# A two-stage sequence model in one launch: norm chains with a joint Ln/Exp table set, norms in pieces, and modulation units at other places

## The reference, cut to what matters

```python
def first_block(x, ...):                      # x: 1 x 256 x 1024
    h = x
    for l in range(DEPTH):                    # DEPTH = 2
        u = _rmsnorm(h, norm_mix_g[l])
        (s_z, s_xbc, s_dt, g_q, ..., gates) = _split(u @ w_in[l], IN_SIZES)
        ...                                   # three branches, gated and merged
        h = h + merged @ w_out[l]
        u = _rmsnorm(h, norm_ffn_g[l])
        up = _dwconv(u @ w_up[l], ffn_conv_w[l], ffn_conv_b[l])
        h = h + (silu(a_half) * v_half) @ w_down[l]
        h = h + (p[l] @ w_ple[l]) * sigmoid(h @ w_ple_gate[l])
    return _rmsnorm(h, final_norm_g)

def second_block(x, c, ...):
    # modulation: sh1, sc1, g1, sh2, sc2, g2 = split(silu(c) @ w_ada + b_ada, 6)
    h = rms_norm(x, norm1_g) * (1 + sc1) + sh1
    ...                                       # differential attention and pooling, out product
    x = x + g1 * mix
    h = rms_norm(x, norm2_g) * (1 + sc2) + sh2
    y = hierarchical_moe(h, ...)              # 32 experts in 4 groups, top 2
    x = x + g2 * y
    return rms_norm(x, final_g)
```

## Time and profile before

| | |
|---|---|
| time, median of 3 runs | 2242.56 us (2238.19 to 2245.31) |
| profiled execution, first to last instruction | 2239.7 us |
| TensorE matmuls busy | 2032.3 us (91%) |
| VectorE busy | 1202.3 us (54%) |
| ScalarE busy | 902.2 us (40%) |
| DMA | 499.45 MB, mean 223 GB/s |
| mean granted clock of TensorE | 0.956 |

### The profile page before, as it was taken

One profiled execution on the slowest core, in us unless ns is written; L12 is line 12 of the kernel. 1 busy time (PEld: TensorE's weight loads), 2 busy tenths in 40 slices (PEclk: granted clock), 3 DMA queues, 4 the chain that ended last, 5 costly groups with the idle time before them and its releaser, 6 DMA issues.

```text
span 2239.7 us, 47727 instructions
## 1 busy us (share of the span) xinstructions
PE 2032.3 (91%) x20606; PEld 1722.9 (77%) x20606; DVE 1202.3 (54%) x2113; ACT 902.2 (40%) x1088; POOL 30.9 (1%) x61
## 2 busy tenths in 40 slices
PE   8999999989999999999999999999897767777775
PEld 7998858889999989988588899999776533343433
DVE  4887856388677557878563886775233200000001
ACT  5554533474555455545334755554312200000001
POOL 0000000000000000000000000000000000000000
PEclk9999999999999999999999999999998898878878
DMA  6554333445445554553334454556662699999996
GB/s 254 183 204 178 132 113 133 160 160 189 169 178 187 202 196 175 208 184 132 114 132 160 160 182 165 182 188 226 249 242 94 276 421 422 422 422 422 422 422 259
DMA packets 70920, 499.45 MB, mean 223 GB/s; under 512 B 8320, under 2 KB 8448, under 8 KB 12016
## 3 DMA queue, kind: packets, MB, share of 16 engines
q1 hardware_dynamic: 66240, 481.41, 56.2%
q0 software_dynamic: 4384, 14.75, 1.9%
q10 hardware_dynamic: 144, 1.05, 0.1%
HBM read 496.03 MB, written 1.15 MB: 222 GB/s over the span
## 4 chain that ended last, share of the span: by engine, by line
PE 69%; DMA 14%; DVE 6%; ACT 5%; SPq 3%; issue 2%; DVEq 0%; ACTq 0%
PE bank L863 25%; PE bank L868 12%; DMA ring<-stream 11%; PE bank L873 9%; DMA arena<-stream 4%; SPq L715 3%; PE bank L1102 3%; PE bank L806 2%; PE bank L851 2%; PE bank L818 2%; PE bank L1320 2%; PE bank L856 1%; PE bank L1217 1%; PE bank L1075 1%; PE bank L924 1%
## 5 line engine op out<-in xcount | busy, mean ns | idle before, releaser
L873 PE MATMUL bank<-u,ring 128*128 128x256 f32 x1152 | 256.2, 381 | 0.0
L2241 DVE TENSOR_TENSOR ring_r<-ring,weights_and_u_split 128x2048 fp32r<-128x2048 f32 x88 | 201.6, 2292 | 94.0 <-ACT weights_and_u_split L1680 90.3
L873 PEld LDWEIGHTS bank<-u,ring 128*128 128x128 f32 x1152 | 216.9, 190 | 30.2 <-issue 0.8
L2556 DVE COPY arena<-bank 128x128 f32<-128x128 f32 x32 | 9.3, 292 | 401.8 <-PE bank L1338 401.8
L868 PE MATMUL bank<-weights_and_u_split,ring_r 128*128 128x256 f32 x1592 | 208.9, 283 | 0.0
L1680 ACT ACTIVATE weights_and_u_split<-ring 128x2048 fp32r<-128x2048 f32 x88 | 167.8, 1908 | 96.5 <-PE bank L868 52.6
L863 PE MATMUL bank<-weights_and_u_split,hidden_and_weights_high 128*128 128x256 f32 x1600 | 202.1, 284 | 0.0
L863 PEld LDWEIGHTS bank<-weights_and_u_split,hidden_and_weights_high 128*128 128x128 f32 x1600 | 195.4, 192 | 4.7 <-issue 4.3
L868 PEld LDWEIGHTS bank<-weights_and_u_split,ring_r 128*128 128x128 f32 x1592 | 199.0, 192 | 0.0
L2241 DVE TENSOR_TENSOR ring_r<-ring,hidden_and_weights_high 128x2048 fp32r<-128x2048 f32 x60 | 137.0, 2287 | 33.5 <-ACT hidden_and_weights_high L1680 33.5
L1320 PE MATMUL bank<-ring,arena 128*32 128x256 f32 x1008 | 90.6, 489 | 58.9 <-DMA ring<-stream 58.9
(11 more groups left out here) (407 smaller groups left out, 3491.8 us busy)
## 6 DMA issues: line engine op xcount, KB each, us to landing
ring<-stream SPq DMA_DIRECT2D x329, 1024.0 KB, 4.8
arena<-stream SPq DMA_DIRECT2D x128, 1024.0 KB, 26.2
arena<-rows_scratch POOLq DMA_DIRECT2D x48, 256.0 KB, 4.1
h<-x_d ACTq DMA_DIRECT2D x1, 1024.0 KB, 5.5
out<-arena SPq DMA_DIRECT2D x1, 1024.0 KB, 3.9
con<-con_d SPq DMA_DIRECT2D x1, 976.5 KB, 12.6
arena<-con_d POOLq DMA_DIRECT2D x1, 848.0 KB, 7.1
par<-par_d POOLq DMA_DIRECT2D x2, 422.0 KB, 4.6
```

The costliest lines, as they stand in the source:

```text
L873: mm = pe.matmul(bank[:, c * S:(c + 1) * S], w[:, k, c * P:(c + 1) * P], x[:, k, :], start=(k == 0), stop=(k == KC - 1))
L2241: tt(ring_r[:, POS[k] % RING, :], w, high(k).bitcast(F32), ALU.subtract).then_inc(wlo_ok.sem, 1)
```

## The change

It has five parts.

1. `prime` no longer computes anything: it loads the table set that holds both Ln and Exp. Neither the dummy nor a load between Ln and Exp is left in the program.
2. x comes in four loads with semaphores of their own. The ring's first load waits for the second of them. The first table load waits for nothing but `eps`.
3. Squares and sums of layer 1's first norm, and of the second block's first norm, are made in pieces among the four pleg units ("next_square", "next_sum"). Of the third norm in the second block two of four sums stand ahead of the last unit. At the end squares follow the h adds by pairs and the output is stored in two DMAs.
4. The weight copy of z0 stands ahead of u's parts, which are an item of their own ("parts").
5. Pair 0 of the modulation units moves behind z1, with SiLU of c behind z0's read, and pair 2 moves from bm's start to the end of the layer, behind the last pleg unit.

```diff
@@ unit_order
-    out, mk, bh, o = [ADA1, ADA1 + 1], OF["mk"], OF["bh"], OF["out"]
+    out, o = [], OF["out"]
...
-        if n == OF["gh"] + 3:
+        if n == OF["z"] + 1:
+            out += [ADA1, ADA1 + 1]
+        elif n == OF["gh"] + 3:
             out += [ADA1 + 2, ADA1 + 3]
-        elif n == bh + 3:
-            out += [ADA1 + 4, ADA1 + 5]
...
-    return out
+    return out + [ADA1 + 4, ADA1 + 5]
@@ sched
-        sched = [("norm", 0), ("ada", 0), ("ada_read", 0), ("split", 1), ("unit", 0), ("ada_cols", 0), ("lb", 0), ("split", 2), ("rows", 0)]
+        sched = [("norm", 0), ("split", 1), ("parts", 0), ("unit", 0), ("lb", 0), ("split", 2), ("rows", 0)]
...
+            if n == 1:
+                sched.append(("silu_c", 0))
             if n == 2:
-                sched.append(("keep_h", 0))
+                sched += [("ada", 0), ("ada_read", 0), ("keep_h", 0)]
+            if n == 3:
+                sched.append(("ada_cols", 0))
...
                 sched.append(("ple_add", n - pleg))
+                if n > pleg:
+                    sched.append(("next_sum", n - pleg - 1))
+                sched.append(("next_square", n - pleg))
+        sched += [("ada", 2), ("ada_read", 2), ("next_sum", 3), ("ada_cols", 2)]
@@ sync
-                    sp.wait_ge(x_in, 16)
+                    sp.wait_ge(x_in[1], 16)
...
-                sp.wait_ge(y2_fin, 2)
-                sp.dma_start(out, flat(0, KC)).then_inc(stored, 16)
-                sp.wait_ge(stored, 16)
+                for n in range(2):
+                    sp.wait_ge(y2_fin, 5 + n)
+                    sp.dma_start(out[:, n * 4 * S:(n + 1) * 4 * S], flat(4 * n, 4)).then_inc(stored, 16)
+                sp.wait_ge(stored, 32)
@@ tensor
+            def norm_sum(lay, before, j):
+
+                pe.wait_ge(sq_ready.sem, sq_ready.at(lay, before + j + 1))
+                for c in (2 * j, 2 * j + 1):
+                    mm = pe.matmul(A[4][:, 0:S], ones, arena[:, SQ + c, :], start=(c == 0), stop=(c == KC - 1))
+                if j == 3:
+                    mm.then_inc(ss_ready.sem, 1)
...
                 out_products(m, heads, False, True)
+                if m > WOUT2:
+                    norm2(3, [m - WOUT2 - 1])
             gemm2(WOUT2 + 3, chunks(O2, KC))
-            norm2(3)
+            norm2(3, (2, 3))
@@ scalar
             def prime():
 
-                act.activation(small[:, 255:256], eps[:, 0:1], ACT.Ln)
+                act.preload_act_table_set("natural_log_exp_and_others")
...
-            act.dma_start(h[:].rearrange("p c s -> p (c s)"), x_d).then_inc(x_in, 16)
+            for j in range(4):
+                act.dma_start(h[:, 2 * j:2 * j + 2, :].rearrange("p c s -> p (c s)"), x_d[:, 512 * j:512 * (j + 1)]).then_inc(x_in[j], 16)
@@ vector
             for c in range(KC):
                 ins = stt(h[:, c, :], A[c // 2][:, c % 2 * S:c % 2 * S + S], mod[:, 40 + c:41 + c], h[:, c, :], ALU.mult, ALU.add)
-            ins.then_inc(y2_fin, 1)
+                if c % 2:
+                    ins.then_inc(y2_fin, 1)
```

More of the change, by code:

```diff
@@ L920, in item @@
                 elif kind == "norm":
-                    for c in range(KC):
-                        if c % 2 == 0:
-                            pe.wait_ge(sq_ready.sem, sq_ready.at(lay, 4 * k + c // 2 + 1))
-                        mm = pe.matmul(A[4][:, 0:S], ones, arena[:, SQ + c, :], start=(c == 0), stop=(c == KC - 1))
-                    mm.then_inc(ss_ready.sem, 1)
+                    for j in range(4 if k or not lay else 0):
+                        norm_sum(lay, 4 * k, j)
+                elif kind == "next_sum":
+                    norm_sum(lay + 1, 0, k)
                 elif kind == "rows1":
@@ L1084, in item, with norm2 @@
                         mm.then_inc(mhT.sem, 1)
-            def norm2(n):
-                for c in range(KC):
-                    if c % 2 == 0:
-                        pe.wait_ge(sq_ready.sem, sq_ready.at(DEPTH, 4 * (n - 1) + c // 2 + 1))
-                    mm = pe.matmul(A[4][:, 0:S], ones, arena[:, SQ + c, :], start=(c == 0), stop=(c == KC - 1))
-                mm.then_inc(ss_ready.sem, 1)
+            def norm2(n, pieces=range(4)):
+                for j in pieces:
+                    norm_sum(DEPTH, 4 * (n - 1), j)
             def gemm2(m, x):
@@ L1690, in norm2 @@
                 x = h[:].rearrange("p c s -> p (c s)")
-                for j in range(4):
-                    if n == 1:
-                        act.wait_ge(h_new.sem, h_new.at(DEPTH - 1, j + 1))
-                        x = flat(PLG, KC)
-                    elif n == 2:
+                for j in range(4 if n > 1 else 0):
+                    if n == 2:
                         act.wait_ge(u_ready.sem, u_ready.at(DEPTH, 2 * j + 2))
@@ L1698, in norm2 @@
                         act.wait_ge(freed[use2(WOUT2 + j)[0]].sem, use2(WOUT2 + j)[1] + 1)
-                    if j == 2:
+                    elif n == 4:
+                        act.wait_ge(y2_fin, j + 1)
+                    if n > 2 and j == 2:
                         prime()
@@ L1832, in _ @@
                 dense()
-            act.wait_ge(y2_fin, 1)
             norm2(4)
@@ L2266, in norm2 @@
                             ins.then_inc(u_ready.sem, 1)
[L2267 to L2268 removed]
+                        if n != 1 and c in (3, KC - 1):
+                            ins.then_inc(y2_fin, 1)
                     return
```

47 lines of the change are left out of this document (25 added, 22 removed).

## The result

The changed kernel takes 2254.93 us, the median of four executions (2252.64 to 2255.91), where the kernel before takes 2240.52 on the same chip (2238.19 to 2245.31). The ratio is 1.0055, with a 95% interval of 1.0038 to 1.0072: slower, and clear of the 0.3% that a measurement can tell. The ratio makes it 12.3 us. The profiled execution, the fastest of its four, has a span of 2250.9 us against 2239.7, so 11.2 us of the loss stand in the traces. The forecast was 2241, with a range up to 2248.

A forecast was written before the change was run, and what follows sets the result against it. TensorE was taken to bound most of the program (69% of the chain), so only its waits could change. -1.3 - 0.9 + 2.3 + 3.4 - 0.6 - 4.1 = -1.2 us, on the median of 2242.56, gave 2241, range 2230 to 2248.

The forecast's parts named there:

- The rival on the other side: Ring of loads set back at three starts, clock falling at each: +7.4 us, 2250, chance 0.12.
- Start of layer 0: Up to z3: u earlier, but most given back as z2's load and the moved pair make TensorE wait: -1.3 us.
- x in quarters: Start of layer 0: first quarter lands no earlier than 3.6 us, so sums start near 4.9 and u 4.1 earlier.
- bm's start: Pair 2 leaves it in both layers; products were hidden, only its columns are gained: -0.9 us for two layers.
- Edge: Between the layers: layer 1's parameter load releases u late, at 804.85, and z3 follows 25.55 behind: +2.3 us.
- Entry: Into the second block: last modulation load lands at 1597.6 against 1592.25, partly offset by table savings: +3.4 us.
- four more at 2.5 each: Entry: after the second modulation unit's load at 1587.8, four further loads land 2.5 us apart, by 1597.6.
- The saving of 1.9 for the tables: Entry: the norm loses its ready-made load and dummy (0.6 net) and the load between Ln and Exp (1.3): -1.9 us.
- Norm ahead of the experts: Second block: last square has less cover, +0.7, and the table load goes, -1.3: -0.6 us.
- End: Last norm and store: sums end 2.1 earlier, no load between Ln and Exp, -1.3, smaller last store, -0.7: -4.1 us.
- the waits don't come: Rival at start, edge and entry: copies, parameters and loads come in time, each place keeps its gain: -11.5, 2231, chance 0.13.
- A switch costs more than its load: Rival at five exposed table switches: each costs 1.3 us beyond its load: -7.7, 2235, chance 0.07.

The follow-up runs named there:

- best: Changed kernel with pairs and layer-end pieces as before, x in one load, layer 1's parameters earlier, constant matmuls at two waits per layer: 2237.2 us, ratio 0.9969.
- best2: The combination in best, with the matmuls of constants only at the first of the two places in each layer: 2229.9 us, ratio 0.9942.
- joint: Kernel before with one edit, prime loads the table set holding both Ln and Exp (also called the joint set alone): 2239.6 us, ratio 0.9986.
- the run without the moves: Changed kernel with both modulation pairs and the layer-end squares and sums where they were before, SiLU of c behind the squares: 2239.1 us, ratio 0.9976.
- jointx4: Kernel before with the joint table set and x in four loads, nothing else: 2239.9 us, ratio 0.9982.

## Why the prediction was wrong

The sign was wrong: -1.2 us forecast, +12.4 measured. The rival on the other side (a chance of 0.12, 2250) had most of the mechanism: loads set back at three starts and the clock falling at each.

**Start of layer 0** (-1.3 forecast, +0.9). The chain was right link by link: u at 12.0 (12.6), a gap of 3.1 us (3.0) ahead of the pair, z3 17.9 us behind z0's end (17.5). z0's end was 25.6 and not 23.8. The step that failed is "x in quarters": it took u's start for what sets z0. What sets it is the second megabyte of the ring, which lands at 14.76, and the copy behind it; with 32 matmuls partly at half clock, z0's end is 1.8 late.

**bm's start** (-0.45 in each layer, +0.6). "The pair's products were hidden" was right, and that made them free. The bounds looked only at gains. Taking away work that fills a wait cannot help and left TensorE idle, after which its clock fell: 3.19 us for 16 matmuls.

**Edge** (+2.3, +6.7). That the parameters would release u was right. Their price was mis-sized: 3.8 to 5.4 us taken from two rows, 6.39 measured here and 8.25 in the run with pair 0 put back. The bound should have come from loads in flight together, 2.5 us for each further megabyte, of which pair 2 releases two just then; those rows were at hand. On top came the clock, which the forecast's own sum left at full and kept for the rival: 5.81 us for the rows unit. Put together, u came 1.5 later than taken (806.4 in the time of the kernel before, for 804.85) and z3 28.4 behind u for 25.55, 2.1 of it in the rows unit: 4.4 in all.

**Entry** (+3.4, +7.4). The last modulation load lands late, as forecast: issued at 1588.96 in the time of the kernel before, which is the 1588.7 of the bound, it takes 9.96 us and lands 6.7 late where 5.3 was taken. The step that was mis-sized is "four more at 2.5 each": the second unit's load landed at 1587.7, as forecast, and the next four 2.6, 2.5, 3.7 and 2.5 behind each other, the last two issued beside each other and a further one, which the forecast had only in its bound of +4.9. The saving of 1.9 for the tables was right in size: the stretch behind the load is 2.1 shorter in best and best2. It did not appear here, because the sums ran at half clock (5.69 us, there 3.73): the stretch took 0.7 more than before and not 1.9 less. The last sum in TensorE's queue ahead of the modulation pair, which gave 3.3 us with the pairs back, cost nothing here, since pair 2 stands ahead of it.

**Norm ahead of the experts** (-0.6, -1.6): better than forecast. The 0.7 us charged for the last square's lost cover did not appear beyond noise; the table load is 1.3 by itself.

**End** (-4.1, -5.1): right, with the store at its bound (2.6 for 3.9 us, where 0.7 was taken) and sums of 5.2 in place of 5.8 us.

**Not foreseen: 1.7 us at 290.** Nothing was edited there. TensorE waits 2.7 us for VectorE in both kernels, and the clock falls behind it in one and not in the other. It fell in this place, in layer 0 or 1 or both, in nine of the fifteen traces other than that of before (those of the fourteen runs and of the changed kernel), and not in that one. In the three traces with the wait filled it fell in neither layer.

The other rivals: "the waits don't come" is refuted at all three places. "A switch costs more than its load" is refuted by the joint set alone. The Trainium skill's drain behind a table load (ScalarE: Activation LUTs, What ACT_TABLE_LOAD costs) is not seen here: in the kernel before, Ln ends at 14.82, the load runs from 14.84 to 16.12 and Exp starts at 16.13. Its 1283 ns are seen. The Trainium skill's fixed 2.0 us of a transfer (DMA: Bandwidth & Descriptors, Anatomy of one DMA), which the page fits to transfers issued by GpSimd, would by an estimate make half of a 3.9 us store 2.95; 2.6 was measured on SyncE, so here the forecast's own bound from rows was nearer.

## What to carry to other kernels

Work that sits in a wait of the engine that bounds a kernel is free twice: it takes no time, and it keeps that engine's clock up. Before moving it, ask what the wait becomes without it, and price the matmuls behind at the lower clock. Whenever a step is moved, list the loads that its end releases and what small, urgent load goes beside them; and whenever a wait is put into a queue, look whether a step behind it is one whose end issues loads. A chain may be shortened only where it ends last: the pieces of the norm were worth nothing in the changed kernel at either edge, while the same idea at the end of the program, where nothing else waits, gave all it promised. And where a change gives nothing at a place, look at the clock there before the saving is called absent: the joint set's 2.1 us at the entry were there in two traces and hidden by half-clock sums in the others.

## What the hardware showed unexpectedly

The granted clock fell behind waits of 1.6 to 5 us in some executions and not in others with the same instructions around: at 290 to 295 it is 0.73 in the changed kernel and 1.00 before, with the same wait of 2.68 us ahead. What decides is open; it was not tried to hold everything else fixed and shift only the time of the wait. It may be what makes the spread of one program, 2233.7 to 2242.8 over ten executions of the run without the moves; only one of the ten has a trace, so that is not shown.

x as four loads of 256 KB made the ring's first four megabytes land 1.6 us later than x as one load of 1 MB, though they were issued 0.3 to 0.4 us earlier (jointx4 against joint, which differ in nothing else). The lateness is in a few parts of each load. A load lands in sixteen parts in the trace, and of the second megabyte thirteen had landed by 13.59 us, as with one load (13.54), but the last at 15.21 and not at 13.62. In the eleven traces with x in four loads this megabyte is complete at 14.0 to 15.6 us, in the five with one load at 13.6 to 13.9. Why the last parts fall behind is open.
